# Expert tiles of a mixture-of-experts layer: rows fetched as half rows, transposed in pairs in the two row halves of TensorE's array, down product put off by one tile

## What is computed

```python
def moe(h, w_router, b_router, w_gate, w_up, w_down):
    # sigmoid router: one of 4 groups of experts, the top 2 of its 4 experts, weights divided by their sum -> combine
    ...
    hid = jax.nn.silu(jnp.einsum('bld,edf->blef', h, w_gate)) * jnp.einsum('bld,edf->blef', h, w_up)
    y = jnp.einsum('blef,efd->bld', hid * combine[..., None].astype(hid.dtype), w_down)
    return y.astype(h.dtype)
```

## Time and profile before

| | us |
|---|---|
| median of 3 runs | 952.81 (952.17 to 958.84) |
| the profiled execution, span from its first to its last instruction | 950.6 |
| layer 0, experts: first gate and up product to the last copy of y | 138.8 to 308.0 |
| layer 1, experts: first gate and up product to the last copy of y | 793.5 to 921.5 |
| PE busy, whole span | 775.6 (82%) |
| DVE / ACT / POOL busy, whole span | 429.6 / 336.3 / 290.3 |

### The profile page before, as it was taken

One profiled execution on the slowest core, in us unless ns is written; L12 is line 12 of the kernel. 1 busy time (PEld: TensorE's weight loads), 2 busy tenths in 40 slices (PEclk: granted clock), 3 DMA queues, 4 the chain that ended last, 5 costly groups with the idle time before them and its releaser, 6 DMA issues. The chain is left out here.

```text
span 950.6 us, 14976 instructions
## 1 busy us (share of the span) xinstructions
PE 775.6 (82%) x5209; PEld 466.6 (49%) x5209; DVE 429.6 (45%) x1039; ACT 336.3 (35%) x776; POOL 290.3 (31%) x694
## 2 busy tenths in 40 slices
PE   0978869999999178999998989989987646999970
PEld 0644425555555024456656666656655333555540
DVE  0039543212122583634765767665844652112116
ACT  0231322322222225534755556464631121322221
POOL 0000112333333100455272735537260012333330
PEclk9989959999999569986998999997997757999995
DMA  9999999999791798657242351523210199999913
GB/s 234 406 375 400 407 382 380 383 366 336 258 378 57 308 362 246 204 157 227 40 117 67 89 140 33 140 44 113 46 50 7 62 408 360 361 379 385 374 69 124
DMA packets 115874, 220.47 MB, mean 232 GB/s; under 512 B 44631, under 2 KB 78751, under 8 KB 104801
## 3 DMA queue, kind: packets, MB, share of 16 engines
q1 hardware_dynamic: 106847, 201.56, 61.0%
q0 software_dynamic: 8224, 15.75, 4.9%
q10 hardware_dynamic: 740, 2.32, 0.8%
HBM read 213.27 MB, written 17.33 MB: 243 GB/s over the span
## 5 line engine op out<-in xcount | busy, mean ns | idle before, releaser
L1200 PE MATMUL banks<-h_cols,weight_ring 128*128 128x512 f32 (+1 forms) x384 | 166.7, 556 | 0.8
L809 DVE TENSOR_TENSOR arena<-arena,banks 128x128 f32<-128x128 f32 x42 | 12.1, 287 | 203.7 <-ACT arena L780 203.7
L867 POOL DMA_INDIRECT y_of_tokens<-arena,place_now x42 | 44.0, 1048 | 169.7 <-ACT arena L787 169.7
L1200 PEld LDWEIGHTS banks<-h_cols,weight_ring 128*128 128x128 f32 x384 | 69.8, 205 | 35.6 <-issue 32.0
L1182 POOL TENSOR_TENSOR arena<-arena 128x60 f32<-128x60 f32 (+10 forms) x240 | 78.7, 328 | 18.8
L1180 POOL TENSOR_TENSOR arena<-arena 128x60 f32<-128x60 f32 (+10 forms) x240 | 76.5, 319 | 18.8
L287 PE MATMUL banks<-weight_ring,c_cols 128*32 128x512 f32 x368 | 53.0, 694 | 27.8 <-DMA weight_ring<-in_w_mod_dram 27.8
L845 POOL DMA_INDIRECT arena<-h_of_tokens,row_now x50 | 49.2, 984 | 85.9 <-DVE place_of_slot L714 38.0
L775 ACT COPY arena<-arena 64x1024 f32<-64x1024 f32 x46 | 48.1, 1045 | 77.1 <-PE banks L733 56.8
L752 PE MATMUL banks<-weight_ring,arena 128*64 128x256 f32 x576 | 67.6, 389 | 1.1 <-ACT arena L775 1.1
L733 PE MATMUL banks<-const,arena 64*128 64x64 f32 x352 | 57.1, 285 | 13.1 <-ACT arena L775 13.1
(11 more groups left out here) (294 smaller groups left out, 1395.2 us busy)
## 6 DMA issues: line engine op xcount, KB each, us to landing
weight_ring<-in_w_mod_dram SPq DMA_DIRECT2D x46, 1024.0 KB, 9.5
weight_ring<-in_dn_w_in_dram SPq DMA_DIRECT2D x32, 512.0 KB, 7.1
weight_ring<-in_w_gate_dram SPq DMA_DIRECT2D x13, 1024.0 KB, 11.1
weight_ring<-in_w_up_dram SPq DMA_DIRECT2D x13, 1024.0 KB, 14.4
weight_ring<-in_w_down_dram SPq DMA_DIRECT2D x13, 1024.0 KB, 16.1
arena<-in_w_gate_dram SPq DMA_DIRECT2D x7, 1024.0 KB, 11.5
arena<-in_w_up_dram SPq DMA_DIRECT2D x7, 1024.0 KB, 14.0
arena<-in_w_down_dram SPq DMA_DIRECT2D x7, 1024.0 KB, 15.4
```

The costliest lines, as they stand in the source:

```text
L867: pool.indirect_dma_start(y_halves, bass.IndirectOffsetOnAxis(m.place_now[:, u:u + 1], 0), v.y_tile[u], None, bounds_check=last_row, oob_i ...
L1200: mm = pe.matmul(bank(6 + j % 2)[:, 0:CTX + SEQ - n0], head_w[h % 2][:, j, k, :], m.hT[:, k, n0:CTX + SEQ], start=(k == 0), stop=(k == KD ...
```

## The change

- A tile's rows are fetched as 128 half rows of 512 numbers (partitions 0 to 63 the first halves, 64 to 127 the second), so `rows_in` and `v.rows` are 128 x 512. Gate and up weights are laid out to match, two runs of 4 KB for a partition in place of one of 8 KB.
- `turn` makes its 8 transpositions in pairs, one in rows 0 to 63 of the array and one in rows 64 to 127, into banks 5 and 6. It stands in one piece behind gate and up.
- The down product of tile q is put off: PE makes it behind gate and up of tile q+1. Its weights are first copied by DVE into a buffer of their own (`down_now`, 128 x 2048), in the same step as the copy of `hidden`. The first tile makes a down product whose result is not used, and one more stands after the loop.
- ACT copies y of tile q-1 in its part for tile q, between SiLU and the copy of rows.
- DVE now loops by expert, with register loads of the counts; the two halves of some layer-norm work (`dve_x`) stand behind the first experts.
- POOL gathers first and scatters then. SP waits for `hidden` in place of `down` ahead of the down weights.

The diff, cut to its core (the declarations of the wider buffers, the tables of indices and the loads of the fifth slot are left out):

```diff
         def sp_gate_up(sp, L, e):
...
-                    sp.dma_start(whole[slot][:, a, :], w.rearrange("(p k) f -> p (k f)", p=P)).then_inc(done, 16)
+                    sp.dma_start(whole[slot][:, a, :].rearrange("p (j n) -> p j n", j=2),
+                                 w.rearrange("(j p k) f -> p j (k f)", j=2, p=P)).then_inc(done, 16)
...
-                sp.wait_ge(s(L.tag + "down"), tb + nt)
+                sp.wait_ge(s(L.tag + "hidden"), tb + nt + 1)
                 sp_down(sp, L, e + EXPERT_SLOTS)
...
-        B_GU, B_HID, B_TURN, B_DOWN = 0, 2, 6, 7
+        B_GU, B_HID, B_TURN, B_DOWN = 0, 2, 5, 7
+        turned_rows = m.ps[:, B_TURN:B_TURN + 2, 0:KD // 2 * TILE]
...
-            def turn(k0, k1):
-                for k in range(k0, k1):
-                    mm = pe.transpose(m.ps[:, B_TURN, k * TILE:(k + 1) * TILE], v.rows[:, k, :], v.ident[0:TILE, 0:TILE])
+            def turn():
+                for k in range(KD // 2):
+                    for h in range(2):
+                        half = slice(h * TILE, (h + 1) * TILE)
+                        mm = pe.transpose(m.ps[:, B_TURN + h, k * TILE:(k + 1) * TILE], v.rows[half, k, :], v.ident[half, half])
                 return mm
...
+            def down():
+                for f in range(FC):
+                    for h in range(2):
+                        mm = pe.matmul(column_half(B_DOWN, h), v.hidden[:, f, :], v.down_now[:, f, h * BANK:(h + 1) * BANK],
+                                       start=(f == 0), stop=(f == FC - 1))
+                mm.then_inc(s(t_ + "down"), 1)
...
-                    turn(0, KD // 2)
+                    turn().then_inc(s(t_ + "turned"), 1)
+
+                    pe.wait_ge(s(t_ + "hidden"), q + 1)
+                    down()
                     pe.wait_ge(s(t_ + "hid_rows"), q + 1)
                     pe.transpose(m.ps[:, B_HID, 0:P], v.hid_rows, v.ident).then_inc(s(t_ + "hid_turned"), 1)
-                    turn(KD // 2, KD).then_inc(s(t_ + "turned"), 1)
...
+            pe.wait_ge(s(t_ + "hidden"), tb + nt + 1)
+            pe.wait_ge(s(t_ + "rows_copied"), tb + nt + 2)
+            down()
...
+            def y_out(n_down, u, stored):
+                act.wait_ge(s(t_ + "down"), n_down)
+                if stored is not None:
+                    act.wait_ge(s(t_ + f"y_stored{u}"), stored)
+                act.copy(v.y_tile[u], m.ps[:, B_DOWN, :]).then_inc(s(t_ + f"y_tile{u}"), 1)
+
+            def tile(j, u, put_out):
                 q = 2 * j + u
                 act.wait_ge(s(t_ + "gate_up"), q + 1)
                 act.activation(v.silu, m.ps[:, B_GU, 0:P], ACT.Silu).then_inc(s(t_ + "silu"), 1)
+                put_out()
                 act.wait_ge(s(t_ + "turned"), q + 1)
                 act.wait_ge(s(t_ + f"rows{u}"), 16 * j + 32)
                 copied(u)
-                act.wait_ge(s(t_ + "down"), q + 1)
...
+            with act.Fori(1, pairs - 1) as j:
+                tile(j + 1, 0, lambda: y_out(2 * j + 3, 1, 16 * j))
+                tile(j + 1, 1, lambda: y_out(2 * j + 4, 0, 16 * j + 16))
+            act.wait_ge(s(t_ + "place_now1"), pairs)
+            y_out(2 * pairs + 1, 1, None)
...
+            def tile(e, q):
                 dve.wait_ge(s(t_ + "silu"), q + 1)
                 dve.tensor_tensor(v.hid_rows, v.silu, m.ps[:, B_GU, P:2 * P], ALU.mult).then_inc(s(t_ + "hid_rows"), 1)
-                dve.wait_ge(s(t_ + "hid_turned"), q + 1)
-                dve.tensor_copy(v.hidden.rearrange("p f n -> p (f n)"), m.ps[:, B_HID, 0:P]).then_inc(s(t_ + "hidden"), 1)
                 dve.wait_ge(s(t_ + "turned"), q + 1)
                 turned()
+                dve.wait_ge(s(t_ + "hid_turned"), q + 1)
+                dve.wait_ge(s(t_ + "down"), q + 1)
+                dve.tensor_copy(v.hidden.rearrange("p f n -> p (f n)"), m.ps[:, B_HID, 0:P])
+                dve.wait_ge(*expert_loaded(L, e))
+                for to, of in down_pieces(expert_slot(L, e)):
+                    ins = dve.tensor_copy(to, of)
+                ins.then_inc(s(t_ + "hidden"), 1)
...
             def pair(j, first=False):
                 for u in range(2):
+                    pool.wait_ge(s(t_ + "rows_copied"), 2 * j + u + 1)
+                    pool.tensor_copy(m.row_now[:, u:u + 1], m.token_of[:, bass.ds(2 * j + u + 2, 1)]
+                                     ).then_inc(s(t_ + f"row_now{u}"), 1)
+                    pool.wait_ge(s("h_stored"), 16 * (L.h_base + L.tiles))
+                    pool.wait_ge(s(t_ + f"row_now{u}"), j)
+                    rows(u, u)
                     if not first:
                         pool.wait_ge(s(t_ + f"y_stored{u}"), 16 * j - 16)
```

More of the change, by code:

```diff
@@ L756, in pe_moe @@
                         after = expert_count(pe, e + 1)
-                    turn(0, KD // 2)
+                    turn().then_inc(s(t_ + "turned"), 1)
+                    pe.wait_ge(s(t_ + "hidden"), q + 1)
+                    down()
                     pe.wait_ge(s(t_ + "hid_rows"), q + 1)
                     pe.transpose(m.ps[:, B_HID, 0:P], v.hid_rows, v.ident).then_inc(s(t_ + "hid_turned"), 1)
-                    turn(KD // 2, KD).then_inc(s(t_ + "turned"), 1)
[L761 to L767, removed]
+                if e + 1 < N_EXPERTS:
+                    nt, tb = after
+            pe.wait_ge(s(t_ + "hidden"), tb + nt + 1)
+            pe.wait_ge(s(t_ + "rows_copied"), tb + nt + 2)
+            down()
         def act_moe(act, L):
@@ L783, in tile @@
                 copied(u)
-                act.wait_ge(s(t_ + "down"), q + 1)
-                if not first:
-                    act.wait_ge(s(t_ + f"y_stored{u}"), 16 * j)
-                act.copy(v.y_tile[u], m.ps[:, B_DOWN, :]).then_inc(s(t_ + f"y_tile{u}"), 1)
             act.wait_ge(s(t_ + "rows0"), 16)
@@ L794, in act_moe @@
             pairs = tile_total(act) // 2
-            tile(0, 0, True)
-            tile(0, 1, True)
-            with act.Fori(1, pairs) as j:
-                tile(j, 0)
-                tile(j, 1)
+            tile(0, 0, lambda: None)
+            tile(0, 1, lambda: y_out(2, 0, None))
+            tile(1, 0, lambda: y_out(3, 1, None))
+            tile(1, 1, lambda: y_out(4, 0, 16))
+            with act.Fori(1, pairs - 1) as j:
[3 more added lines that the diff above has]
+            y_out(2 * pairs + 1, 1, None)
         def dve_moe(dve, L):
@@ L816, in dve_moe @@
             tag = ("ln0a_", "ln1a_")[L.n]
-            for n in range(L.tiles - 2):
+            ahead = L.tiles // 2
+            for n in range(ahead):
                 dve_x(dve, tag, n, L.x_tiles[n], n)
-            if L.tiles == 2:
-                dve_x(dve, tag, 0, L.x_tiles[0], 0)
+            if L.n > 0:
+                dve.sem_inc(s(t_ + "hidden"), 1)
             dve.wait_ge(s("turned_first"), L.n + 1)
             turned()
-            total = tile_total(dve)
-            tile(0)
-            n = L.tiles - (2 if L.tiles > 2 else 1)
@@ L826, in dve_moe @@
-            dve_x(dve, tag, n, L.x_tiles[n], n)
-            tile(1)
-            if n + 1 < L.tiles:
-                dve_x(dve, tag, n + 1, L.x_tiles[n + 1], n + 1)
-            with dve.Fori(2, total) as q:
-                tile(q)
+            nt, tb = expert_count(dve, 0)
+            for e in range(N_EXPERTS):
+                with dve.Fori(0, nt) as i:
+                    tile(e, tb + i)
+                    if e + 1 < N_EXPERTS:
+                        after = expert_count(dve, e + 1)
+                if e + 1 < N_EXPERTS:
+                    nt, tb = after
+                n = ahead + e // 2
+                if n < L.tiles:
+                    dve_x(dve, tag, n, L.x_tiles[n], n, (e % 2,))
@@ L2230, in _ @@
             dve.memset(m.c_cols[:, :, 2:COL], 0.0).then_inc(s("columns"), 1)
+            dve.memset(m.arena[:, 13312:14336], 0.0).then_inc(s(L0.tag + "hidden"), 1)
             dve.memset(m.sums[:, :, :], 0.0).then_inc(s("columns"), 1)
```

49 lines of the change are left out of this document (21 added, 28 removed).

## The result

| | before | after |
|---|---|---|
| median of four runs, us | 952.49 (952.17 to 958.84) | 975.02 (971.49 to 977.58) |
| the profiled execution, time and span | 950.6 (span) | 977.58, span 975.8 |
| PE / DVE / ACT / POOL busy | 775.6 / 429.6 / 336.3 / 290.3 | 765.1 / 479.2 / 313.4 / 296.3 |
| layer 0, first SiLU to last SiLU | 144.53 to 303.95 | 140.73 to 310.68 |
| layer 1, first SiLU to last SiLU | 799.61 to 917.47 | 813.49 to 938.75 |

The ratio is 1.0217, 95% interval [1.018, 1.0253]: slower by 2.2%, 20.7 us on 952.5. The direction and the mechanism were forecast; the forecast size was 3.3%.

The account below looks back on a forecast made before the run. The prediction took PE's own sequence to bound the loops before, and a PE-ACT ring after. Span 950.6 + 26.0 (loops) + 5.0 (starts and ends) = 981.6, plus 2.2 for the median: about 984 us, 3.3% slower, range 974 to 1002.

Parts of the forecast that it names:

- What bounds the loop: Expert loops before the change: PE's own sequence bounds them, busy 151.49 of 154 and 109.17 of 111 us.
- the ring: Every tile: PE down, ACT y, ACT rows, next PE gate and up wait in turn; PE idle about 1.05 us.
- The period: One tile in the expert loops, from gate and up's weight load: 7.58 us against 6.93, growing by 0.65.
- the pairs: PE's eight transpositions as four pairs: 0.58 us per tile; rival that pairs gain nothing: 1.02 us, chance 0.06.
- the copy of rows starts 0.03 later: On ACT, the rows copy starts 0.03 us after y's copy ends and takes 0.62, together 0.65.
- 40 equal periods: Both loops: 23 + 17 periods between first and last tile, each 0.65 us longer, +26.0 us.
- Ends: End of each layer: ACT's last y waits for POOL's copy of `place_now` behind its gather, +3.8 us.
- Starts: Start of each layer: two shorter copies of rows and quicker first transpositions, -1.3 us.
- DVE's copy of weights: DVE copies 128x2048 down weights within SBUF: 1.2 us, bound 2.29, costing nothing in the loop.
- Weights, gathers, clock: Loop rivals: weights or gathers late, up to +10 us, chance 0.05; clock falling to 1.2 GHz, +250, chance 0.02.
- The sum: Whole kernel: 950.6 + 26.0 for loops + 5.0 for starts and ends = 981.6 us of span.

Follow-up runs that it names:

- e1: Changed kernel, ACT copies rows before it waits for the down product and copies y, PE's waits adapted; 935.77 us, ratio to the kernel before 0.9801.
- e4: Changed kernel, ACT's copy of y cut to 128 of 512 columns; 976.47 us with 44 tiles, 962.2 less two periods.
- e6: Changed kernel, POOL copies `place_now` ahead of its gather; 973.46 us in one run.
- e7: Changed kernel, DVE copies only 64 of the 2048 columns of down weights; 1002.07 us with 46 tiles, 972.3 less four periods.
- e5: Kernel before with only half rows and paired transpositions, no put-off down product or DVE weight copy; 946.64 us, ratio 0.9926.

## Why the prediction was right and where it failed

- **What bounds the loop; the ring.** Right. PE 1.02 us idle in each tile (1.05 forecast), released by L786; e1 takes the ring away and the loss with it, e4 moves it by the length of y's copy.
- **The period, 7.58 forecast, 7.45 measured.** This is the first step that failed. Gate and up with the first weight load was put at 3.68 and takes 3.61; the pairs 0.58 and 0.62; down to ACT's y 1.99 and 2.06; the weight load behind the copy of rows 0.10 and 0.06. These cancel (-0.07 + 0.04 + 0.07 - 0.04 = 0). What remains is the term "the copy of rows starts 0.03 later": it starts 0.48 us behind the start of y, while y takes 0.59. ACT's two copies overlap by 0.11, where a pause of 0.03 was assumed. That is 0.13 to 0.14 a tile, over 40 periods 5.4 us. The Trainium skill states the overlap for a neighbouring case: ScalarE: Activation LUTs, section "What ACT_TABLE_LOAD costs", says that ACTIVATEs back to back overlap by about 93 ns. The trace's 0.11 for two copies agrees, and the prediction should have used it.
- **40 equal periods.** Also failed. The first tile of a layer has no y to copy, so its ring is open: 6.35 us. The next three take 7.37. In them y's copy starts 1.98 us behind the start of down, as forecast, in the later ones 2.06. These three stand ahead of ACT's loop; inside it, as ACT's order of instructions shows, a register instruction (L791) takes the wait for `down` ahead of the copy of y. That this costs the 0.08 is not tested. Two first periods cost 2 x 1.1 = 2.2 us less than the others, and six of 7.37 another 0.5. 2 x 6.35 + 6 x 7.37 + 32 x 7.445 = 295.2, against 40 x 6.93 = 277.2: +18.0, measured 17.9, forecast 26.0. The kernel has `put_out` empty for the first tile (`tile(0, 0, lambda: None)`); the sum did not carry it.
- **Ends.** Right in mechanism: the last y waited for POOL's `place_now` behind its gather. +3.8 each was forecast, +3.9 and +4.6 measured; in layer 0 three DVE instructions of 1.22 us run beside POOL, and its gather there took 1.36 in place of 1.03. e6 shows that the next thing behind it, the last down product, is only 1.1 us away in layer 1 and 1.8 in layer 0.
- **Starts.** The sign was right. -1.3 each was forecast from shorter copies and transpositions; measured from the common mark it was -4.0 and -2.1, but these terms gave less than forecast, and the rest is not theirs. From ACT's first copy of rows to the first gate and up it is 3.43 before and 2.82 after in layer 0 (135.32 to 138.75, 132.53 to 135.35), 3.37 and 2.39 in layer 1 (790.17 to 793.54, 806.05 to 808.44): -0.6 and -1.0 are what the copies and transpositions gave. In layer 1 the second copy was to give 0.43 and gave 0.16, since PE now waits for DVE's copy of the transposed rows, 0.69. Most of the rest goes with the granted clock. The first gate and up to its SiLU fell from 5.78 to 5.38 and from 6.07 to 5.05, with a mean granted clock of 0.64 and 0.68, 0.61 and 0.73. In layer 0 another 1.7 lie ahead of the first gather (23.40 from the mark to it before, 21.70 after), in DVE's router work behind PE; PE's product ahead of DVE's table took 1.93 us before and 1.13 after, and from 120 to 124 us the granted clock was 0.50 before and 0.79 after. The last 1.3 lie between that gather and ACT's first copy of rows, while ACT is still at copies for the modulation, a table load and a small SiLU. But for one DVE instruction less in the table (0.1 us), none of these 3.4 and 1.1 us is in work that the change shortened.
- **The middle.** +4.7 between the layers was not forecast. It lies in lines that are the same in both kernels, and the nine profiles spread over 7.4 us there. What sets it is not shown.
- **DVE's copy of weights.** Right: 1.22 us (1.2 forecast), and nobody waits for it in the loop (e7's period; PE's 3.2 us are the two ends). Only at a layer's end does it stand on the way: PE's last down product waits 1.60 us for it.
- **The pairs.** Right in size: eight in 0.62. They are a term of the ring, so by its sum they do shorten the period here; no run shows the changed kernel without them. e5 shows that without the put-off product they give 0.13 of the 0.44.
- **Weights, gathers, clock.** None of these rivals came: no group of gate and up waits for a load, ACT's 17.0 us for a gather are a single wait ahead of layer 1's first tile, the DMA share is 0.83 in layer 0's loop and 0.98 in layer 1's, and with PE busy 86% the granted clock stayed at 1.00, 2.4 GHz, in both stretches. By the Trainium skill's passage that the prediction weighed (TensorE: Matmul & The Clock Gate, "A second HAM failure mode: psum-queue depth-cycling") it might have swung; with PE idle 1.02 us in each tile it did not.
- **The sum.** Forecast +31.0 (26.0 loops, 5.0 starts and ends). Measured in the profiles: 17.9 in the loops, 8.5 at the ends and -6.1 at the starts, together +20.3, beside 20.7 by the ratio of the runs. That these agree is in part luck: of the -6.1 only -1.6 is in the terms that the prediction named, with which the sum is 24.8, and the middle's spread is larger than the gap. What the prediction had wrong is the loops: 26.0 forecast, 17.9 measured, 5.4 of it from the overlap of ACT's two copies and 2.7 from the first tiles.

## What to carry to other kernels

- When a product is put off by a tile, look on every engine for what now stands behind a wait for it. Here the copy that feeds the next tile came to stand behind the copy that waits for the put-off product, and a 0.6 us copy became a ring through three engines. Exchanging two statements turned +2.2% into -2.0%.
- Shortening PE work inside a chain of SiLU, product and copy gives only what the chain leaves (0.13 of 0.44 us in e5). Work from another tile has to stand in that gap first.
- A period times a count can over-size a change. Write the first tiles and the last out by themselves, and take copies in a row on one engine start to start from the trace, not as durations plus a pause.

## What the runs showed of the hardware that was not expected

- Two independent copies in a row on ACT, 0.59 (out of PSUM) and 0.62 us (within SBUF), start 0.48 us apart: they overlap by 0.11 us. With y's copy at 0.27 us the starts are 0.17 apart (205.54 and 205.71).
- Transpositions in the two row halves run beside each other whether they alternate in the program or stand in two blocks of four (0.62 and 0.63 us for eight, the partners 3 and 13 ns apart).
- POOL's indirect DMA instruction ends late when it starts beside a copy within SBUF on DVE. In the changed kernel a scatter from 210.40 takes 1.12 us and ends 0.91 behind the end of DVE's copy (209.39 + 1.22 = 210.61); in e4 it starts at 206.62, 0.32 earlier against that copy, takes 0.31 longer and ends 0.90 behind its end (205.93 + 1.22 = 207.15). Started earlier, it is not done earlier. Every scatter that starts beside that copy does so, 40 in the changed kernel and 42 in e4: it ends 0.88 to 0.92 us behind the copy's end. In e7, without the long copy, the mean is 1.03. The prediction left this rule of the Trainium skill (SBUF — State Buffer, "SBUF: two separate sides", an exclusive lock) out of its sum for want of a row; the trace now agrees with it, and its price here is 0.1 us a tile on an engine with room. The trace of the kernel before already had such a meeting, which the prediction overlooked, with a DVE instruction that is no copy; the gather took 1.71 us in place of 0.97 and ended 0.86 behind it:

```profile
782.98 1.27 DVE L386 SCALAR_TENSOR_TENSOR x_rows<-x_rows,small,ln_vectors 128x1024 f32<-128x1024 f32 x1
783.40 1.71 POOL L845 DMA_INDIRECT arena<-h_of_tokens,row_now  x1 [16.48 <-DVE place_of_slot L714]
```
